# Scan sweep of a state-space mixer: seven VectorE steps and one TensorE sum in another order

## The reference, cut to what matters

```python
def step(h, inp):                        # one chunk, one direction
    qq, kk, vv, aa = inp
    cs = jnp.cumsum(aa, axis=1)
    ...
    y_intra = jnp.einsum('bjlgh,blghp->bjghp', qk[..., None] * decay, vv)
    y_inter = jnp.einsum('bjgn,bghnp->bjghp', qq, h) * jnp.exp(cs)[..., None]
    tail = jnp.exp(cs[:, -1:] - cs)
    h_new = h * jnp.exp(cs[:, -1])[..., None, None] + jnp.einsum('blgn,blghp->bghnp', kk, vv * tail[..., None])
    return h_new, y_intra + y_inter

y = y * jax.nn.silu(z)                   # z: the gate, a part of the input projection
yg = yg * lax.rsqrt(jnp.mean(yg * yg, axis=-1, keepdims=True) + EPS)   # one norm per group
y = yg * norm_g;  return y @ w_out
```

## Time and profile before

| | us |
|---|---|
| median of three timed executions | 1667.93 (1666.49 to 1668.30) |
| the profiled execution's own time | 1666.88 |
| its span, first to last instruction | 1665.1 |
| TensorE busy in the span | 1646.1 (99%) |
| VectorE busy | 1165.7 (70%) |
| ScalarE busy | 798.4 (48%) |
| GpSimd busy | 214.2 (13%) |

### The profile page before, as it was taken

One profiled execution on the slowest core, in us unless ns is written; L12 is line 12 of the kernel. 1 busy time (PEld: TensorE's weight loads), 2 busy tenths in 40 slices (PEclk: granted clock), 3 DMA queues, 4 the chain that ended last, 5 costly groups with the idle time before them and its releaser, 6 DMA issues.

```text
span 1665.1 us, 21246 instructions
## 1 busy us (share of the span) xinstructions
PE 1646.1 (99%) x8278; PEld 1335.5 (80%) x8278; DVE 1165.7 (70%) x1678; ACT 798.4 (48%) x1370; POOL 214.2 (13%) x245
## 2 busy tenths in 40 slices
PE   9999999999999999999999999999999999999998
PEld 6877878788888888888888888776688888888887
DVE  5586874985668787664238998899984788666324
ACT  5475752552254554443224454777752554444221
POOL 0442100442110011110000000132200011111000
PEclk9999999999999999999999999999999999999999
DMA  6211223234321332333332333455333233233332
GB/s 235 93 64 61 76 77 126 92 91 87 77 100 62 104 101 90 101 98 101 92 95 83 101 96 110 153 152 152 102 102 105 73 102 97 93 101 89 101 92 73
DMA packets 55108, 166.53 MB, mean 100 GB/s; under 512 B 6816, under 2 KB 10144, under 8 KB 54880
## 3 DMA queue, kind: packets, MB, share of 16 engines
q1 hardware_dynamic: 51024, 158.80, 30.0%
q0 software_dynamic: 1536, 2.10, 1.1%
q10 hardware_dynamic: 2448, 4.27, 0.8%
HBM read 160.82 MB, written 2.23 MB: 98 GB/s over the span
## 4 chain that ended last, share of the span: by engine, by line
PE 90%; DVE 7%; ACT 1%; issue 1%; DMA 0%; ACTq 0%; DVEq 0%
PE bank L439 25%; PE bank L441 24%; PE bank L440 24%; PE bank L456 2%; PE bank L458 2%; PE bank L457 2%; DVE cv L2415 1%; PE bank L2509 1%; PE bank L2493 1%; PE bank L2481 1%; DVE w_lo L402 1%; DVE a_lo L808 1%; DVE x L703 1%; PE bank L1611 1%; ACT a_hi L771 1%
## 5 line engine op out<-in xcount | busy, mean ns | idle before, releaser
L402 DVE TENSOR_TENSOR w_lo<-raw,w_hi 128x1024 fp32r<-128x1024 f32 (+1 forms) x257 | 328.5, 1284 | 330.3 <-ACT w_hi L395 329.9
L439 PE MATMUL bank<-a_hi,w_hi 128*128 128x512 f32 x1384 | 555.5, 401 | 2.8 <-DVE a_lo L591 2.1
L441 PE MATMUL bank<-a_hi,w_lo 128*128 128x512 f32 x1384 | 539.3, 390 | 0.0
L440 PE MATMUL bank<-a_lo,w_hi 128*128 128x512 f32 x1384 | 538.9, 389 | 0.0
L395 ACT ACTIVATE w_hi<-raw 128x1024 fp32r<-128x1024 f32 (+1 forms) x259 | 267.9, 1041 | 315.9 <-DMA raw<-in_w_down 142.4
L439 PEld LDWEIGHTS bank<-a_hi,w_hi 128*128 128x128 f32 x1384 | 259.9, 188 | 69.9 <-issue 13.5
L440 PEld LDWEIGHTS bank<-a_lo,w_hi 128*128 128x128 f32 x1384 | 260.0, 188 | 58.5 <-issue 6.7
L441 PEld LDWEIGHTS bank<-a_hi,w_lo 128*128 128x128 f32 x1384 | 259.8, 188 | 54.9
L1491 ACT ACTIVATE u<-bank,par 128x512 f32<-128x512 f32 x88 | 68.5, 779 | 176.3 <-DVE bank L855 176.3
L1534 POOL TENSOR_TENSOR gv<-u 128x512 f32<-128x512 f32 x44 | 57.3, 1303 | 579.3 <-DVE u L1510 579.3
L439 PE MATMUL bank<-g_hi,w_hi 128*128 128x512 f32 x308 | 119.8, 389 | 0.0
(11 more groups left out here) (428 smaller groups left out, 2487.2 us busy)
## 6 DMA issues: line engine op xcount, KB each, us to landing
raw<-in_w_up SPq DMA_DIRECT2D x86, 512.0 KB, 3.7
raw<-in_w_in SPq DMA_DIRECT2D x50, 512.0 KB, 3.7
raw<-in_w_out SPq DMA_DIRECT2D x32, 512.0 KB, 3.6
raw<-in_w_down SPq DMA_DIRECT2D x32, 512.0 KB, 3.5
raw<-in_w_xbc SPq DMA_DIRECT2D x23, 512.0 KB, 3.7
back<-cum_rows SPq DMA_DIRECT2D x32, 256.0 KB, 4.0
em<-cum_rows SPq DMA_DIRECT2D x32, 256.0 KB, 5.0
raw<-in_w_z SPq DMA_DIRECT2D x16, 512.0 KB, 4.3
```

Source lines behind the costliest of these rows:

```text
L402: nc.vector.tensor_tensor(lo_of(q)[:, 0:w], raw_of(q)[:, 0:w], hi_of(q)[:, 0:w].bitcast(F32), ALU.subtract).then_inc(lo_done, 1)
L439: nc.tensor.matmul(out, wh, rhs_hi[:, k, :], start=k == first, stop=False)
L440: nc.tensor.matmul(out, wh, rhs_lo[:, k, :], start=False, stop=False)
L441: return nc.tensor.matmul(out, wl, rhs_hi[:, k, :], start=False, stop=stop)
```

## The change

On VectorE, in every group: the low part of gate tile 4g+3's slot moves from ahead of `grow(g, 1)` to behind `carry(g, 0)`; `take_z(4g+2)` moves from ahead of `fed(g, 1)` to behind `fed(g, 2)`; the low part of tile 4g+4's slot moves from ahead of `grow(g, 2)` to behind that `take_z`. From group 2 on, `normed_y(g-2, 3)` moves from ahead of `tailed(g, 1)` to behind `join(g, 2, 3)`, in the last group behind one low part more. On TensorE, `norm_sum(g-1)` moves behind the two gate parts that followed it; in the last group there are none, and it stays. No operation is added or taken away.

```diff
             between(g, 2)
-            if g:
-                norm_sum(g - 1)
             for i in range(4):
...
                 if i == 0 and not last:
                     part_z(*first)
                     part_z(*second)
+                if i == 0 and g:
+                    norm_sum(g - 1)
                 carried(g, i)
...
                 take_z(4 * g + 1)
-                if g > 1:
-                    normed_y(g - 2, 3)
             tailed(g, 1)
-            lo_to(dve, z0 + 4 * g + 3)
             grow(g, 1)
             carry(g, 0)
-            take_z(4 * g + 2)
+            lo_to(dve, z0 + 4 * g + 3)
             fed(g, 1)
             join(g, 0, 1)
             tailed(g, 2)
-            lo_to(dve, z0 + 4 * g + 4)
             grow(g, 2)
             carry(g, 1)
             fed(g, 2)
+            take_z(4 * g + 2)
+            lo_to(dve, z0 + 4 * g + 4)
             join(g, 2, 3)
+            if g > 1 and not last:
+                normed_y(g - 2, 3)
             if last:
                 weigh(g, 0)
                 carry(g, 2)
                 weigh(g, 1)
                 lo_to(dve, z0 + 4 * g + 5)
+                normed_y(g - 2, 3)
```

## The result

The changed kernel takes 1671.67 us (median of 11 runs, 1670.07 to 1672.67), against 1667.65 (11 runs, 1665.58 to 1668.64) for the kernel before on the same chip. The ratio is 1.0023, with a 95% interval of 1.0015 to 1.0031: slower by some 3.8 us (2.5 to 5.2 by the interval; the medians lie 4.0 apart), where 2.75 were forecast. The time alone doesn't exclude the forecast; what tells more are the stages of the profile.

A forecast was written before the change was run, and what follows sets the result against it. The prediction took TensorE, busy for 99% of the span, as the bound. Terms of 1.1 (group 0), 0.7 + 0.2 (group 1), 0.1 (group 2) and 0.65 (group 3) made 1667.93 + 2.75 = 1670.7 us; range 1667.3 to 1672.8.

The forecast's parts named there:

- L2493's waits gone: In the sweep, TensorE's waits for `hst` at `between`, 2.9 us in four, would be gone or nearly.
- L439 waiting for `w_lo` in groups 1, 2 and 3: Gate tiles 4g+3 would wait on TensorE for their moved low part, 0.6 to 1.3 us each.
- `norm_sum` free: Moving `norm_sum` behind two gate parts would cost nothing, since ScalarE reads the sum 4.4 us after it has ended.
- Group 0: `take_z` and a low part behind `fed(0, 2)` would make `inside` late, with no `hst` wait to win: +1.1 us.
- Group 1: Gate tile's low part late, 0.7 us with restart, plus 0.2 behind `fed(1, 2)`, where `norm_sum` had covered 0.9 of 1.1.
- Group 2: Late low part 1.3 us and stretch behind `fed(2, 2)` 0.8, against 2.0 lost before: +0.1 us.
- Group 3: The normalisation now stands ahead of `low(0)`, for which the first `out3` step waits: +0.65 us.
- The step ahead of it: In group 3, VectorE was taken as the bound up to `carry(3, 2)`, with the same work reordered, so that point stays unmoved.
- The wait of gate tile 15: In group 3, the gate tile's moved low part would be 0.85 us late, 0.45 less than in group 2.
- the signs of being wrong: No L439 wait in group 2, group 0's `inside` not late, or GpSimd's holds at steps other than `tailed` and `grow`.
- slower by more: Rival: GpSimd holds one more VectorE operation in groups 1, 2 and 3, 1.1 us each: 1674.0, 1671.8 with one; 30 in 100.
- Faster: Rival: low parts of 4g+3 are in time, so waits of 4.2 us go: 1665.7, or 1664; 8 in 100.

The follow-up runs named there:

- low3_back: The changed kernel with the low part of gate tile 4g+3 put back ahead of `grow(g, 1)`; ratio 0.9996 to the kernel before.
- gate_late_only: The kernel before with only `take_z(4g+2)` and the low part of tile 4g+4 moved behind `fed(g, 2)`; ratio 1.0010 to the kernel before.
- group3_old: The changed kernel with VectorE's steps of the last group in the order of before; ratio 1.0012 to the kernel before.
- low3_only: The kernel before with only the low part of gate tile 4g+3 moved behind `carry(g, 0)`; ratio 1.0005 to the kernel before.
- norm_late_only: The kernel before with only `normed_y(g-2, 3)` moved, as the change does; ratio 0.9988 to the kernel before.
- after_again: The changed kernel, unaltered, profiled once more; 1672.53 us in one run, beside 1668.39 for one run of the kernel before.

## Why the prediction was right, and where its size was off

The sign, the places and, but for group 3, the mechanism came out: L2493's waits gone, L439 waiting for `w_lo` in groups 1, 2 and 3, L2502 and L2509 late in group 0, `norm_sum` free. By its steps:

- **Group 0**, +1.1: measured +1.05 in every profile with the two steps behind `fed(0, 2)`, and 0 in every one without. This chain had no operation without a row and no GpSimd in it.
- **Group 1**, 0.7 + 0.2: measured +1.19. `grow` was held once, as counted, but the low part met GpSimd's third addition (1.48 us for 1.21) and was costed there at its free duration, though that of group 2 was not. The wait shows 0.94, and the gate tile's second pass comes 1.18 later than before: the restart costs 0.24 and not the 0.1 that the prediction gave it. The 0.2 behind `fed(1, 2)` is there, at `inside(1, 0)`, which starts 0.73 us behind `carried(1, 0)` where it was 0.52. Against it stands what the prediction left out: before, the pair of `between(1, 2)` was itself a slow one (1.98 for 1.88), hindered by a wait too short to be shown, and starting it without delay gives back 0.15. 1.18 - 0.15 + 0.2 = 1.2. In low3_back and gate_late_only the last two cancel, so group 1 there comes out even.

TensorE in group 1, before and then after:

```profile
1098.40 1.98 PE L2493 MATMUL bank<-hst,xbc 128*128 128x512 f32 x4
1103.86 0.60 PE L2502 MATMUL bank<-cst,y 128*128 128x128 f32 x4
1104.38 1.09 PE L2509 MATMUL bank<-em,xtok 128*64 128x128 f32 x16
```

```profile
1100.23 1.88 PE L2493 MATMUL bank<-hst,xbc 128*128 128x512 f32 x4
1105.57 0.60 PE L2502 MATMUL bank<-cst,y 128*128 128x128 f32 x4
1106.30 1.09 PE L2509 MATMUL bank<-em,xtok 128*64 128x128 f32 x16
```

- **Group 2**, 1.3 + 0.8 against 2.0: the wait for the low part shows 1.28 and costs 1.52 with its restart; the stretch behind `fed(2, 2)` costs 0.88 (0.27 at L2502, where no wait of note is shown, and 0.61 at L2509, which shows 0.54); the vanished stalls of L2493 give back 2.18. In sum +0.22, measured +0.21.
- **Group 3**, +0.65: the mis-sized term, +1.92. The normalisation ahead of `low(0)` costs 0.66, as said. The step ahead of it was "up to `carry(3, 2)` VectorE does the same work as before in another order ... so I take that point as unmoved". It lacked, first, that VectorE's start in the group isn't fixed. It came 0.70 us later, and the late `tailed(3, 0)` met a whole gate multiplication of GpSimd (2.41 us, 1.91 before): 1.2 in all. Second, its reason is wrong. The work isn't the same, since the normalisation (1.30 us with its hold) has left this stretch; and VectorE isn't the bound all the way, since at `fed(3, 2)` it now idles 1.28 us for `states(3, 2)`, which TensorE brings late because gate tile 15 has waited 1.59 for its low part:

```profile
1188.67 0.69 DVE L2766 TENSOR_TENSOR hst<-hst,bank 128x512 f32<-128x512 f32 x1 [1.11 <-PE bank L2481]
1189.52 0.69 DVE L2766 TENSOR_TENSOR hst<-hst,bank 128x512 f32<-128x512 f32 x1 [0.17 <-PE bank L2481]
```

That the two come out equal, so that the point stays (30.49 us in the changed kernel and in group3_old), is luck. low3_back, with the same moves but this low part ahead of `grow`, has no idle time there and reaches `carried(3, 0)` 28.98 us behind the group's begin, 1.5 earlier, at an entry of 5.49.

- The wait of gate tile 15 was put at 0.85 us late and is 1.59, from the same late start. The prediction's sum left it out; by low3_back it is worth 1.5 us of the group.
- Of the signs of being wrong one was met in part: GpSimd also holds the low part itself, in groups 1, 2 and 3 (some 0.27 each), and the prediction had counted that for group 2 only.

The rival "slower by more" thus has part of its case: one partial hold more in group 1 (0.3) and half a hold in group 3. By the number alone the measured 1671.67 lies nearer to its 1671.8, for one hold more, than to the forecast 1670.7. "Faster" failed on the very step that it named, the low part's readiness in group 2.

Steps don't add. The low part alone adds 0.25 us to the sweep and 0.05% to the time, but 3.6 us and 0.27% on top of the others. Alone it takes the place of the L2493 stall; once `take_z`, a low part and the normalisation have left that stretch there is no stall left for it to replace.

Is the late entry into group 3 chance, or does the change cause it? All eight profiles with `take_z(4g+2)` behind `fed(g, 2)` have 5.3 us or more there (5.33 to 5.88), and of the six without, four have 4.71, one 4.81 and one 6.04. So the order seems to favour it, beside what varies by itself. What goes with it is how long the load for the last head takes: 5.48 to 6.04 us from issue to use in the nine profiles with a late entry, 4.62 to 4.90 in the other five. The time of its issue alone isn't the cause: low3_only issued it 9.57 us ahead of the group's begin, as the late ones did (9.56 to 9.88), and entered at 4.81. Why the load takes longer with these orders stays open. It bears on some 1.3 us of the 3.8.

## What to carry to other kernels

Before a step is moved behind others, look up on the waiting engine's program, not on its own, who wants it first: a gate tile's low part was wanted 3 us before the state that it was made to yield to. Move what nobody waits for soon, and leave the rest; two such steps gained as much (0.23%) as the whole change lost. Where a shift of under 2 us decides, take two profiles of the same kernel before a group's length is read as the work of the order.

## What the runs showed of the hardware

- What a hold by GpSimd costs can be worked out. In group 2 of the changed kernel the two held 128x512 steps of VectorE with both inputs in SBUF ended 0.55 us after the addition that they met (1130.70 after 1130.15, 1133.00 after 1132.45), and the low part 1.08 after its (1135.60 after 1134.52): each runs almost whole once GpSimd is done, 0.13 us short of its free 0.68 or 1.21. The price is thus the rest of the addition less 0.13: 1.1 us where VectorE starts 0.3 to 0.5 us into it, 0.27 where it meets the end. Cutting the additions from 512 columns to 8 gave back 1.08, 1.06 and 0.27 us. The Trainium skill (SBUF — State Buffer, "SBUF: two separate sides") says that the two engines lock each other out for a whole instruction; the runs agree. It names VectorE's two-port performance modes as a second case beside two inputs in SBUF, which the prediction's "only" leaves out; no run here shows that case.
- The same 256 KB load of rows over the partitions took 4.71 us from issue to use in one execution and 6.36 in another of the same kernel. The sweep of an unaltered kernel so differs by 0.9 us (before) and 1.5 us (after) between profiles, while group 0, which nothing late reaches, agrees to 0.01; group 1 of norm_late_only, in the order of before, took 43.43 for 43.00.
- A wait of TensorE costs more than it shows. At a gate tile's first matmul it was 0.24 us more, whatever the wait's length: the next pass came 1.18 us later beside a wait of 0.94 (after, group 1), 1.47 beside 1.23 (after_again), 0.99 beside 0.75 (low3_only) and 1.52 beside 1.28 (after, group 2). 0.16 of it is hidden by the row of the pass before, which lasts 0.59 us where the next could start after 0.43. Waits below that don't show as waits at all, as the 0.15 in group 1 of the kernel before.
